# Reordering TensorE's small steps within an expert of a mixture-of-experts layer

## The reference

```python
def moe(h, lp):
    xt = h.reshape(B * T, D)
    logits = (xt @ lp['router_w'] + lp['router_b']).astype(jnp.float32)
    top_v, top_i = lax.top_k(logits, TOP_K)
    top_w = jax.nn.softmax(top_v, axis=-1)
    combine = jnp.sum(jax.nn.one_hot(top_i, N_EXPERTS) * top_w[..., None], axis=1)
    out = jnp.zeros((B * T, D), jnp.float32)
    for e in range(N_EXPERTS):
        gu = xt @ lp['expert_w_gu'][e] + lp['expert_b_gu'][e]
        glu = jnp.minimum(gu[:, :D_FF], SWIGLU_LIMIT)
        lin = jnp.clip(gu[:, D_FF:], -SWIGLU_LIMIT, SWIGLU_LIMIT)
        act = glu * jax.nn.sigmoid(SWIGLU_ALPHA * glu) * (lin + 1.0)
        out = out + combine[:, e:e + 1] * (act @ lp['expert_w_down'][e] + lp['expert_b_down'][e])
    return out
```

## Time and profile before

| | us |
|---|---|
| median of 3 runs | 1395.98 |
| lowest and highest run | 1394.65, 1396.06 |
| the profiled execution, its time | 1394.64 |
| the profiled execution, its span (first to last instruction) | 1392.9 |
| TensorE busy | 1268.3 (91%) |
| VectorE busy | 340.8 (24%) |
| ScalarE busy | 254.9 (18%) |
| GpSimd busy | 31.1 (2%) |
| DMA over the span | 462.42 MB, mean 332 GB/s |

### The profile page before, as it was taken

One profiled execution on the slowest core, in us unless ns is written; L12 is line 12 of the kernel. 1 busy time (PEld: TensorE's weight loads), 2 busy tenths in 40 slices (PEclk: granted clock), 3 DMA queues, 4 the chain that ended last, 5 costly groups with the idle time before them and its releaser, 6 DMA issues.

```text
span 1392.9 us, 17218 instructions
## 1 busy us (share of the span) xinstructions
PE 1268.3 (91%) x6853; PEld 596.7 (43%) x6853; DVE 340.8 (24%) x757; ACT 254.9 (18%) x429; POOL 31.1 (2%) x74
## 2 busy tenths in 40 slices
PE   4898999999999999989999999899999998999996
PEld 2676889878633333333333333333333333333332
DVE  0558962323421111111111111211111112111113
ACT  2340123110321121111211111111111211112112
POOL 3000110001000000000000000000000000000000
PEclk8999999889999999999999999999999999999999
DMA  9968311257479999999999999999999999999990
GB/s 325 323 217 303 116 31 33 91 189 268 151 307 409 398 403 417 388 410 403 402 411 400 404 394 411 409 405 405 410 407 381 405 414 405 412 401 409 412 372 30
DMA packets 65451, 462.42 MB, mean 332 GB/s; under 512 B 7687, under 2 KB 30894, under 8 KB 40846
## 3 DMA queue, kind: packets, MB, share of 16 engines
q1 hardware_dynamic: 63102, 457.67, 82.6%
q0 software_dynamic: 944, 3.03, 0.6%
q10 hardware_dynamic: 1376, 1.31, 0.3%
HBM read 460.66 MB, written 1.33 MB: 332 GB/s over the span
## 4 chain that ended last, share of the span: by engine, by line
PE 84%; DVE 10%; ACT 2%; DMA 2%; issue 2%; SPq 1%; DVEq 0%
PE bank L1200 32%; PE bank L1232 17%; PE bank L1241 5%; PE bank L606 4%; PE bank L1146 4%; PE bank L631 3%; PE bank L1183 2%; PE bank L1042 2%; PE bank L1079 2%; PE bank L1222 2%; DVE corr L2001 2%; DVE pmT L2006 2%; DVE pmT L2004 2%; DMA ring<-in_w_mod 2%; DVE gate L1998 2%
## 5 line engine op out<-in xcount | busy, mean ns | idle before, releaser
L1200 PE MATMUL bank<-ring,gate 128*64 128x512 f32 x2048 | 451.9, 594 | 0.0
L1200 PEld LDWEIGHTS bank<-ring,gate 128*64 128x64 f32 x2048 | 144.2, 137 | 300.1 <-issue 300.1
L1232 PE MATMUL bank<-ring,pmT 128*64 128x512 f32 x1024 | 233.6, 610 | 27.5 <-DVE pmT L2006 27.5
L1998 DVE TENSOR_SCALAR gate<-bank 128x512 f32<-128x512 f32 x32 | 22.1, 692 | 769.3 <-PE bank L1200 769.3
L1232 PEld LDWEIGHTS bank<-ring,pmT 128*64 128x64 f32 x1024 | 74.8, 140 | 164.2 <-issue 164.2
L1241 PE MATMUL bank<-kk 64*128 64x512 f32 x256 | 63.6, 611 | 25.1 <-ACT kk L1554 25.1
L1533 ACT ACTIVATE raw<-bank 128x512 f32<-128x512 f32 x33 | 19.7, 597 | 340.8 <-PE bank L1146 340.8
L1554 ACT ACTIVATE kk<-bank 128x512 f32<-128x512 f32 x32 | 19.1, 597 | 308.2 <-PE bank L1232 308.2
L1146 PE MATMUL bank<-bt,vt 128*64 128x512 f32 x264 | 62.3, 592 | 0.0
L631 PE MATMUL bank<-hnT,ring 128*128 128x256 f32 x240 | 56.6, 392 | 4.6 <-issue 4.6
L606 PE MATMUL bank<-hnT,ring 128*128 128x256 f32 x256 | 55.9, 379 | 0.0
(11 more groups left out here) (352 smaller groups left out, 1033.8 us busy)
## 6 DMA issues: line engine op xcount, KB each, us to landing
ring<-in_expert_w_gu SPq DMA_DIRECT2D x128, 2048.0 KB, 9.9
ring<-in_expert_w_down SPq DMA_DIRECT2D x64, 2048.0 KB, 9.7
ring<-in_w_mod SPq DMA_DIRECT2D x24, 1024.0 KB, 9.9
ring<-in_w_in SPq DMA_DIRECT2D x17, 1024.0 KB, 8.0
ring<-in_w_o SPq DMA_DIRECT2D x4, 1024.0 KB, 9.5
ring<-in_w_pool_out SPq DMA_DIRECT2D x2, 1024.0 KB, 6.8
ring<-in_w_rwkv_out SPq DMA_DIRECT2D x2, 1024.0 KB, 11.6
pr<-gate_rows POOLq DMA_DIRECT2D x4, 512.0 KB, 8.3
```

The source lines that it names most:

```text
L1200: last = mm(b[h * SLOTS:(h + 1) * SLOTS, :], xg[:, 2 * (u % 2) + i, u // 2, :], w[:, i, o + h * 512:o + (h + 1) * 512], start=False, stop= ...
L1232: last = mm(G[h * SLOTS:(h + 1) * SLOTS, :], actT[:, i, u, :], w[:, i, h * 512:(h + 1) * 512], start=False, stop=(u == DN_UNITS - 1 and i ...
L1998: v.tensor_scalar(gsb, banks[4][:, :], LIMIT, None, ALU.min).then_inc(S("g_ready"), 1)
```

## The change

TensorE's order within a pass becomes: up-projection in one piece; gather of the next item; selection transposes; down bias; activations' transposes; gather transposes; down-projection; the linear half of the next item's up bias; scatter; the gate half of the up bias. ScalarE's order follows: sigmoid, copy of the gather, copy of the selection transposes, copy of the gather transposes, copy of the down-projection. `up_bias` now takes a bank and a row of biases. No instruction and no semaphore is added or removed; VectorE's and SyncE's programs are as they were.

```diff
@@ -1175,19 +1175,19 @@
         pe.wait_ge(S("xgt_ready"), 1)
         gather_turn()
 
-        def up_bias():
-
-            for b, r in ((G, 0), (L, 2)):
-                for h in range(2):
-                    q = slice((r + h) * NE, (r + h + 1) * NE)
-                    mm(b[h * SLOTS:(h + 1) * SLOTS, :], sele[q, :], bgu[q, :], start=True, stop=False)
+        def up_bias(b, r):
+
+            for h in range(2):
+                q = slice((r + h) * NE, (r + h + 1) * NE)
+                mm(b[h * SLOTS:(h + 1) * SLOTS, :], sele[q, :], bgu[q, :], start=True, stop=False)
 
         pe.wait_ge(S("bgu_in"), 64)
         pe.wait_ge(S("bdn_in"), 32)
         pe.wait_ge(S("sele_ready"), 1)
         pe.wait_ge(S("items_ready"), 1)
         n_items = pe.value_load(item[0:1, ITEMS:ITEMS + 1], min_val=NE, max_val=NE + EXTRA)
-        up_bias()
+        up_bias(L, 2)
+        up_bias(G, 0)
         with pe.Fori(0, n_items) as it:
 
             pe.wait_ge(S("xg_ready"), it + 1)
@@ -1200,12 +1200,9 @@
                             last = mm(b[h * SLOTS:(h + 1) * SLOTS, :], xg[:, 2 * (u % 2) + i, u // 2, :], w[:, i, o + h * 512:o + (h + 1) * 512],
                                       start=False, stop=(u == GU_UNITS - 1 and i == 1))
                 last.then_inc(S("chunk_used"), 1)
-                if u == 1:
-                    pe.wait_ge(S("sel_ready"), it + 2)
-                    gather()
-
-            pe.wait_ge(S("xgt_ready"), it + 2)
-            gather_turn()
+
+            pe.wait_ge(S("sel_ready"), it + 2)
+            gather()
             pe.wait_ge(S("pw_ready"), it + 1)
             for s in range(NS):
                 last = tr(banks[7][:, s * T:(s + 1) * T], pw[:, s, :], ident[:])
@@ -1221,6 +1218,8 @@
             for i in range(4):
                 last = tr(L[:, i * P:(i + 1) * P], act_[:, i::4], ident[:])
             last.then_inc(S("actT_done"), 1)
+            pe.wait_ge(S("xgt_ready"), it + 2)
+            gather_turn()
 
             pe.wait_ge(S("actT_ready"), it + 1)
             for u in range(DN_UNITS):
@@ -1233,6 +1232,8 @@
                                   start=False, stop=(u == DN_UNITS - 1 and i == 3))
                 last.then_inc(S("chunk_used"), 1)
 
+            pe.wait_ge(S("sele_ready"), it + 2)
+            up_bias(L, 2)
             pe.wait_ge(S("pwt_ready"), it + 1)
             pe.wait_ge(S("ysb_ready"), it + 1)
             for s in range(NS):
@@ -1241,8 +1242,7 @@
                     last = mm(banks[2 * s + h][:, :], pwt[r, s, :], ysb[r, :], start=False, stop=True, skip_group_check=True)
                 last.then_inc(S(("scattered_ctx", "scattered_lat")[s]), 1)
 
-            pe.wait_ge(S("sele_ready"), it + 2)
-            up_bias()
+            up_bias(G, 0)
 
 
     @block.scalar
@@ -1543,12 +1543,12 @@
         n_items = act.value_load(item[0:1, ITEMS:ITEMS + 1], min_val=NE, max_val=NE + EXTRA)
 
         with act.Fori(0, n_items) as it:
-            gathered_out(it + 2)
             act.wait_ge(S("g_ready"), it + 1)
             af(sgb, gsb, ACT.Sigmoid, scale=ALPHA).then_inc(S("sg_ready"), 1)
-            gather_turn_out(it + 2)
+            gathered_out(it + 2)
             act.wait_ge(S("pwt_done"), it + 1)
             af(pwt.rearrange("p s t -> p (s t)"), banks[7][:, 0:TT], ACT.Copy).then_inc(S("pwt_ready"), 1)
+            gather_turn_out(it + 2)
 
             act.wait_ge(S("chunk_used"), it * NU + NU)
             af(ysb, banks[4][:, :], ACT.Copy).then_inc(S("ysb_ready"), 1)
```

## The result

The changed kernel takes 1343.54 us (median of 4 runs, 1340.59 to 1345.17) against 1395.32 us beside it: a ratio of 0.9634, 95% interval 0.9606 to 0.9662. Its profiled execution took 1343.58 us, span 1341.8.

What follows compares the result with a forecast made beforehand. Bound: TensorE's own work plus uncovered waits. -1.72 + 0.25 + 0.16 = -1.31 us a pass, -41.9 over 32 passes, and -6.8 for the clock gave 1345.9 profiled, 1347 as median; range 1338 to 1360.

Steps and rivals of the forecast that it cites:

- The gather's place: Gather's 8 instructions moved from between the up-projection's halves to behind it: -1.72 us a pass for everything starting at R.
- R: The release of the last up-projection matmul in a pass, from which the prediction counts its times.
- What stands behind R: Gather, selection transposes and down bias after the up-projection: activations' transposes start at R+3.04 instead of R+2.79, 0.25 us late.
- The lower bound of 0.05: Least lateness of the activations' transposes: 0.05 us if the down bias costs only 0.86 and changes of shape nothing.
- Gather transposes in the wait: Behind the activations' transposes, R+3.62 to R+4.36, while VectorE copies: cost nothing, or 0.6 us without that cover.
- ScalarE's table load: One load at the loop's head, run before the wait for gsb, in place of two a pass: taken as 0.
- Rival D: Table load falls between the wait for gsb and the sigmoid: 0.35 us more a pass, 1358 us; chance 0.05.
- The split bias: Lin half of the up bias in the 0.78 us wait ahead of the scatter: scatter 0.16 us late, bounds 0 to 0.35.
- The clock: Four 3.4 us stretches at 1.2 GHz in the loop go as the gap's idle time shrinks to a fifth: -6.8 us.
- Rivals A and C: Slow-clock stretches stay, 1354 us, chance 0.07; or the clock falls in every pass, 1402 us, chance 0.02.
- DMA: Weight transfers need 29.4 us a pass at 428 GB/s, within 0.3 us of the bound; 16 us of lag can build up.
- Rival B: DMA replaces TensorE as the bound, with the present 30.93 us a pass as ceiling: 1372 us; chance 0.05.

Runs made afterwards that it cites:

- the two fills of the kernel before: Kernel before with about 0.7 us of idle matmuls, or five idle transposes, ahead of the activations' transposes: 1387.69 us (0.9958) and 1386.87 us (0.9949).
- that variant: Changed kernel with the gather back between the up-projection's units and the up bias whole behind the scatter: 1411.11 us, ratio 1.0125.
- the run that reached 429 GB/s: Kernel with whole up bias and late selection transposes, minus the second half of the fourth unit's up-projection matmuls, same bytes: 1322.19 us, ratio 0.9481.

## Why the prediction was right

**The gather's place.** Right in size: R comes 1.72 us earlier after the start of the up-projection, and with the gather put back the pass is 31.07 us. It is the whole gain of the pass.

**What stands behind R.** Right, and slightly over: forecast 0.25 us late, measured 0.18. The transposes came at R+1.60 to the hundredth. The selection transposes and the change of shape before the bias took 0.37, where 0.42 was taken: the 0.13 for that change is the one term that stands in no row, although the text says that each does. The step behind the bias took 1.00 for 1.02. The lower bound of 0.05 was worked out wrong: 1.60, 0.29 and 0.86 are 2.75, before VectorE's 2.79, so the bound is 0. The 1334 in the range goes with 0; with 0.05 it would be 1335.5.

**Gather transposes in the wait.** Right: free where they are, 0.68 us a pass where they are not covered, and 22.6 us between the two medians.

**ScalarE's table load.** Right: one load a pass, straight behind the eviction, off the chain. Rival D did not happen.

**The split bias.** Right: 0.16 us late forecast, 0.15 measured; undone, the kernel gains 4.8 us. Added to the kernel before it cost 9.6 us, 4.6 by itself and the rest through the clock. That second part was in no step of the prediction.

**The clock.** Right that the four stretches go. The reason given, that idle time goes out of the gap, is borne out by the two fills of the kernel before. That none at all was left is in part luck, for the argument went by the amount of idle time alone. With 1.77 us of it (0.42, 0.97 and 0.38) in place of 1.81 and the same pass length there were eighteen stretches, and the part without matmuls was as long as before. Nothing in the prediction looked at when the gap comes. Rivals A and C, drops that stay or multiply, did not happen in the changed kernel. Their condition, that transposes count for nothing, is against the fill with transposes; but drops that become more frequent by an edit of the gap exist, and that variant is 17.5 us slower than the kernel before.

**DMA.** Right that it is near and not the bound: the floor of 29.35 us a pass is real, and so is the lag that the ring can take. Rival B falls with the run that reached 429 GB/s for most of the loop. The slack was sized well too: 16 us of lag on top of 10.2 to landing was the estimate, and TensorE waits on the ring once a unit lands 25 us after its issue.

**The sum.** The pass changed by -1.40 for a forecast -1.31 (-1.72, +0.18, +0.15, and -0.01 behind the scatter), 2.9 us over 32 passes. Against it the loop's first up bias began 0.57 us later in this execution (386.23 for 385.66). 1345.9 was forecast for the profiled execution and 1343.6 came. The 1.3 us that the prediction added for the median over the profiled execution did not show (1343.54 and 1343.58); so 1347 was 3.5 us too high, 2.3 of it through the sum.

## What to carry to other kernels

When an engine must wait for another, list its own small steps with their inputs' times and put into the wait those that fit: here 1.72 us of gather moved from in front of the release to behind it made the pass 1.54 us shorter (31.07 to 29.53), 49 us over 32 passes. Then measure each filler against its wait: the half bias of 1.00 us in a wait of 0.75 lost time, because alone it cost what the whole did. A deep ring lets the compute engine run a little below the transfers' floor for a loop of bounded length, so compare the lag over the whole loop with the slack, not the rates of one pass.

## What the runs showed of the hardware

In four kernels the gap behind the up-projection held two or three idle pieces below 1 us each, 1.8 us together in a pass of 31. TensorE then went to 1.2 GHz for 3.4 us at regular steps, in 4, 7, 7 or 18 places of the loop. At 30.93 us a pass the number depended on where in the gap the idle pieces lay, at 31.07 it did not. The changed kernel (0.38 us idle there), the one with late gather transposes (0.86) and the one with five more transposes (0.26 and 0.86) had no such stretch. Filling 0.7 us of the gap with unused work, matmuls or transposes alike, removed all of them and made the kernel 0.4 to 0.5% faster.

Four bias instructions on two groups of 32 rows take as long as eight on four groups (1.07 and 1.09 us); a change of the stationary operand's shape goes with about 0.1 us between two streams (0.53 between starts for 0.43).

One queue kept 429 GB/s over 900 us, with a median of 25 us between issue and landing in its later part.
